# Inner feed-forward groups with the weights stationary and both parts of x moving

## The reference

```python
def rms_norm(x, g):
    y = xf * lax.rsqrt(jnp.mean(xf * xf, axis=-1, keepdims=True) + EPS)
    return (y * g.astype(jnp.float32)).astype(x.dtype)

def swiglu(h, w_gate, w_up, w_down):
    return (jax.nn.silu(h @ w_gate) * (h @ w_up)) @ w_down

    f = swiglu(rms_norm(x, g[0]), w_ffn_gate[layer, 0], ...)
    x = x + 0.5 * rms_norm(f, g[1])
...
    hn = rmsnorm(h, norm2_g[l])
    h = h + jnp.square(jax.nn.relu(hn @ w_ff1[l])) @ w_ff2[l]
```

## Time and profile before

| | before |
|---|---|
| median of 3 runs | 1413.6 us (1412.82 to 1416.67) |
| span of the profiled execution | 1415.0 us (the page gives no other time for it) |
| PE / weight loads busy | 1381.6 / 1130.3 us (98% / 80%) |
| DVE / ACT busy | 808.2 / 682.4 us (57% / 48%) |
| chain that ended last | PE 95%, ACT 3%, DVE 1%, issue 1% |
| DMA | 247.09 MB, 175 GB/s |

### The profile page before, as it was taken

How to read it: one execution, slowest core, us unless ns; L and a number is a source line. 1 busy time by engine, 2 the same in 40 slices (tenths; PEclk the granted TensorE clock), 3 DMA queues, 4 the chain that set the end, 5 groups by cost and what they waited for, 6 DMA issues and landing times.

```text
span 1415.0 us, 17379 instructions
## 1 busy us (share of the span) xinstructions
PE 1381.6 (98%) x6524; PEld 1130.3 (80%) x6524; DVE 808.2 (57%) x886; ACT 682.4 (48%) x873; POOL 36.8 (3%) x100
## 2 busy tenths in 40 slices
PE   6999999999999999999999999999999999999997
PEld 4888888888888888888877788888787678888886
DVE  4444567674455655454568755446676457665543
ACT  5344455454444554433467643445663455553442
POOL 1000000000000000000001100000000000000000
PEclk9999999999999999999999999999999989999999
DMA  7555655546656554565651365555543243565540
GB/s 255 201 184 197 200 190 184 188 144 196 195 179 223 178 185 143 188 197 181 237 184 55 119 199 187 187 199 202 186 177 120 70 171 120 179 222 194 178 163 30
DMA packets 160156, 247.09 MB, mean 175 GB/s; under 512 B 9006, under 2 KB 104424, under 8 KB 160104
## 3 DMA queue, kind: packets, MB, share of 16 engines
q1 hardware_dynamic: 159824, 246.28, 52.3%
q10 hardware_dynamic: 280, 0.10, 0.0%
HBM read 245.30 MB, written 1.05 MB: 174 GB/s over the span
## 4 chain that ended last, share of the span: by engine, by line
PE 95%; ACT 3%; DVE 1%; issue 1%; POOL 0%; DMA 0%; ACTq 0%; POOLq 0%; DVEq 0%
PE GU L527 15%; PE GU L529 15%; PE GU L528 15%; PE DD L527 11%; PE DD L529 11%; PE DD L528 11%; PE GU L592 4%; PE TB L564 3%; PE GU L599 2%; PE TB L720 2%; PE GU L1178 1%; ACT xh L1443 1%; ACT whi L1431 1%; PE DD L1148 0%; DMA sg<-in_hgrn_norm_g 0%
## 5 line engine op out<-in xcount | busy, mean ns | idle before, releaser
L2005 DVE TENSOR_TENSOR wlo<-raw,whi 128x2048 fp32r<-128x2048 f32 (+1 forms) x226 | 513.9, 2282 | 271.3 <-ACT whi L1431 271.2
L1431 ACT ACTIVATE whi<-raw 128x2048 fp32r<-128x2048 f32 (+1 forms) x226 | 429.9, 1909 | 175.8 <-PE DD L529 166.5
L527 PE MATMUL GU<-whi,xh 128*128 128x512 f32 (+1 forms) x944 | 373.0, 395 | 2.9 <-DVE hid L2122 2.9
L529 PE MATMUL GU<-whi,xl 128*128 128x512 f32 (+1 forms) x944 | 367.5, 389 | 0.0
L528 PE MATMUL GU<-wlo,xh 128*128 128x512 f32 (+1 forms) x944 | 366.5, 388 | 0.0
L527 PEld LDWEIGHTS GU<-whi,xh 128*128 128x128 f32 x944 | 177.7, 188 | 39.3 <-issue 4.9
L529 PEld LDWEIGHTS GU<-whi,xl 128*128 128x128 f32 x944 | 177.6, 188 | 37.4
L528 PEld LDWEIGHTS GU<-wlo,xh 128*128 128x128 f32 x944 | 177.8, 188 | 34.6
L527 PE MATMUL DD<-whi,hth 128*128 128x512 f32 x496 | 194.7, 393 | 0.0
L529 PE MATMUL DD<-whi,htl 128*128 128x512 f32 x496 | 193.2, 390 | 0.0
L528 PE MATMUL DD<-wlo,hth 128*128 128x512 f32 x496 | 193.1, 389 | 0.0
(11 more groups left out here) (276 smaller groups left out, 1087.4 us busy)
## 6 DMA issues: line engine op xcount, KB each, us to landing
raw<-in_w_ffn_gate SPq DMA_DIRECT2D x88, 512.0 KB, 4.0
raw<-in_w_ffn_up SPq DMA_DIRECT2D x88, 512.0 KB, 4.9
raw<-in_w_ffn_down SPq DMA_DIRECT2D x88, 512.0 KB, 4.3
raw<-in_w_ff SPq DMA_DIRECT2D x64, 512.0 KB, 4.2
raw<-in_w_in SPq DMA_DIRECT2D x40, 512.0 KB, 4.5
raw<-in_w_conv_in SPq DMA_DIRECT2D x24, 512.0 KB, 4.8
raw<-in_w_kv SPq DMA_DIRECT2D x16, 512.0 KB, 4.7
raw<-in_w_conv_out SPq DMA_DIRECT2D x8, 512.0 KB, 4.8
```

What stands on the lines that cost most here:

```text
L527: pe.matmul(dst, h, w_h, start=start, stop=False)
L529: return pe.matmul(dst, l, w_h, start=False, stop=stop)
L1431: nc.scalar.activation(whi[s][:, 0:size], raw[s][:, 0:size], ACT.Copy).then_inc(hi_done[s], 1)
L2005: nc.vector.tensor_tensor(wlo[s][:, 0:size], raw[s][:, 0:size], whi[s][:, 0:size].bitcast(F32), ALU.subtract).then_inc(lo_done[s], 1)
```

## The change

In groups 1 to 9 of stages 1 to 4 and 1 to 6 of ff the operands change places. A 128x128 piece of the weight tile is stationary, and x moves. `xh` and `xl` now lie side by side in one tensor `xhl`, so that one matmul of 512 columns makes high x high and high x low at once (two sums of 256 columns in one bank), and a second one of 256 columns adds low x high. The hidden channels come out on the partitions, in four quarters of 128 channels: the two banks `GU` (gate) and the two banks `TB` (up). DVE adds each bank's two halves with a reduce over pairs. The hidden values thus are transposed already; `hidden_transposes` remains for group 0 only, and in the last group those of its own values (`tail_transposes`).

The row factor now would be a factor for each column. For the gate it is needed before silu: DVE spreads it (`row_scales`), PE transposes it in step 1 (`row_transposes`), DVE copies it to SBUF (`row_copy`), and `wide_hidden` multiplies with it. For up it is left out, and comes in where DD is read (`rhalf`, the scale of ACT's Square); in ff its square does (`rsq`, relu commutes with it). `hth` is written from `hid` in SBUF when the previous down projection has ended (`wide_hi`, `wide_lo`).

```diff
-        xh = sb("xh", [P, KT, S], F32R)
-        xl = sb("xl", [P, KT, S], F32R)
+        xhl = sb("xhl", [P, KT, 2, S], F32R)
+        xh, xl = xhl[:, :, 0, :], xhl[:, :, 1, :]
...
+                quarter = [GU[:, 0, :], GU[:, 1, :], TB[:, 0, :], TB[:, 1, :]]
...
+                def row_transposes():
+
+                    n.row += 1
+                    pe.wait_ge(spread_ready, n.row)
+                    for t in range(TT):
+                        mm = pe.transpose(DD[:, 0, t * P:(t + 1) * P], spread[:, t, :], ident[:, :])
+                    mm.then_inc(row_ready, 1)
+
+                def wide(f, e, half):
+
+                    wh, wl, cs = view(whi[e.slot], e), view(wlo[e.slot], e), slice(f * P, (f + 1) * P)
+                    for k in range(4):
+                        kk = 4 * half + k
+                        pe.matmul(quarter[f], wh[:, k, cs], xhl[:, kk, :, :].rearrange("p a n -> p (a n)"),
+                                  start=(kk == 0), stop=False)
+                        mm = pe.matmul(quarter[f][:, 0:S], wl[:, k, cs], xh[:, kk, :], start=False, stop=(kk == 7))
+                    return mm
...
                     for b, e in enumerate(es):
-                        pe.wait_ge(t_used[b], d + t0[b] + g + 1)
+                        if g == 0:
+                            pe.wait_ge(t_used[b], t0[b] + 1)
+                        else:
+                            pe.wait_ge(ht_lo[b], d + wide0[b] + g)
...
-                def step(g, at, d=0, static=True):
-
-                    es = ent[at:at + per]
-                    if g == 1:
-                        x_half(gu_banks, es[0], 0, 0, False, read=(gu_used, gu0 + 1), rows=True)
-                    else:
-                        for t in range(TT):
-                            pe.wait_ge(gu_used[t], d + gu0 + g)
-                        x_half(gu_banks, es[0], 0, 0, False, d=d)
-                    hidden_transposes(g - 1, d)
-                    x_half(gu_banks, es[1], 1, 4, True, d=d, done=gu_ready)
-                    down(g - 1, es[2:], d, start=(static and g == 1))
+                def step_1(at):
+
+                    e0, e1, *ds = ent[at:at + per]
+                    pe.wait_ge(gu_used[0], gu0 + 1)
+                    for e in (e0, e1):
+                        pe.wait_ge(lo_done[e.slot], e.raw_before + 1)
+                    wide(0, e0, 0)
+                    wide(0, e1, 1)
+                    hidden_transposes()
+                    if nd == 1:
+                        row_transposes()
+                    pe.wait_ge(gu_used[1], gu0 + 1)
+                    wide(1, e0, 0)
+                    wide(1, e1, 1).then_inc(gu_ready, 1)
+                    for b in range(nd):
+                        pe.wait_ge(t_used[b], t0[b] + 1)
+                    wide(2, e0, 0)
+                    wide(2, e1, 1)
+                    wide(3, e0, 0).then_inc(used[e0.slot], 1)
+                    wide(3, e1, 1).then_inc(used[e1.slot], 1)
+                    if nd == 1:
+                        pe.wait_ge(row_used, n.row)
+                    down(0, ds, 0, start=True)
+
+                def step(g, at, d=0):
+
+                    e0, e1, *ds = ent[at:at + per]
+                    pe.wait_ge(gu_used[0], d + gu0 + g)
+                    pe.wait_ge(lo_done[e0.slot], d + e0.raw_before + 1)
+                    wide(0, e0, 0)
+                    wide(1, e0, 0)
+                    pe.wait_ge(gu_used[1], d + gu0 + g)
+                    wide(2, e0, 0)
+                    wide(3, e0, 0).then_inc(used[e0.slot], 1)
+                    pe.wait_ge(lo_done[e1.slot], d + e1.raw_before + 1)
+                    wide(0, e1, 1)
+                    wide(1, e1, 1).then_inc(gu_ready, 1)
+                    wide(2, e1, 1)
+                    wide(3, e1, 1).then_inc(used[e1.slot], 1)
+                    down(g - 1, ds, d, start=False)
...
-                    hidden_transposes(g - 1, 0)
...
+                step_1(base + 2)
...
+                                     ACT.Square, scale=rcol(FFN_PRE[i], t) if i in FFN_PRE else 1.0,
...
+                def wide_hi(g, ds, d=0):
+
+                    for b, e in enumerate(ds):
+                        act.wait_ge(used[e.slot], d + e.split_before + 1)
+                        act.wait_ge(ht_ready[b], d + wide0[b] + g)
+                        nc.scalar.activation(hth[:, 2 * b:2 * b + 2, :].rearrange("p k n -> p (k n)"), hid[:, b, :],
+                                             ACT.Copy).then_inc(ht_hi[b], 1)
+
+                def wide_gate(g, d):
+
+                    if nd == 1:
+                        act.wait_ge(zg_ready, d + wide0[0] + g)
+                        nc.scalar.activation(sg[:, 0, :], sg[:, 1, :], ACT.Silu).then_inc(silu_done, 1)
...
-                        nc.scalar.activation(sg[:, t, :], GU[:, t, :], ACT.Relu,
-                                             scale=rcol(pre, t)).then_inc(gu_used[t], 1)
...
+                        nc.scalar.activation(sg[:, t, :], GU[:, t, :], ACT.Relu).then_inc(gu_used[t], 1)
...
-                    for q in range(nd):
-                        split(ent[e + q], d)
-                    hidden_hi(g - 1, d)
+                    if g == 1:
+                        for q in range(nd):
+                            split(ent[e + q], d)
+                        hidden_hi()
+                    else:
+                        wide_hi(g - 1, ent[e - per:e - per + nd], d)
+                        for q in range(nd):
+                            split(ent[e + q], d)
                     split(ent[e + nd], d)
-                    gate(g, d)
+                    wide_gate(g, d)
                     split(ent[e + nd + 1], d)
...
-                    ins = nc.vector.scalar_tensor_tensor(out=tmp[:, t, cs], in0=DD[:, 2 * t + nn, :], scalar=HALF[i],
+                    ins = nc.vector.scalar_tensor_tensor(out=tmp[:, t, cs], in0=DD[:, 2 * t + nn, :],
+                                                         scalar=rhalf[:, t:t + 1] if i in FFN_PRE else HALF[i],
                                                          in1=gain[:, i % 2, cs], op0=ALU.mult, op1=ALU.mult)
...
+                def wide_lo(g, d=0):
+
+                    for b in range(nd):
+                        dve.wait_ge(ht_hi[b], d + wide0[b] + g)
+                        nc.vector.tensor_tensor(htl[:, 2 * b:2 * b + 2, :].rearrange("p k n -> p (k n)"), hid[:, b, :],
+                                                hth[:, 2 * b:2 * b + 2, :].rearrange("p k n -> p (k n)").bitcast(F32),
+                                                ALU.subtract).then_inc(ht_lo[b], 1)
+
+                def wide_sum(dst, banks, done):
+
+                    return nc.vector.tensor_reduce(dst.rearrange("p (f n) -> p f n", f=2),
+                                                   banks[:, :, :].rearrange("p f (a n) -> p f n a", a=2), AX.X, ALU.add)\
+                        .then_inc(done, 1)
+
+                def wide_hidden(g, d):
+
+                    dve.wait_ge(gu_ready, d + gu0 + g + 1)
                     if nd == 1:
-                        dve.wait_ge(sg_done[t], d + sg0 + g + 1)
-                        nc.vector.scalar_tensor_tensor(out=hid[:, t, 0:FG], in0=GU[:, t, FG:512], scalar=rcol(pre, t),
-                                                       in1=sg[:, t, 0:FG], op0=ALU.mult, op1=ALU.mult)\
+                        wide_sum(sg[:, 1, :], GU, gu_used[0])
+                        dve.wait_ge(gu_used[0], d + gu0 + g + 1)
+                        z = sg[:, 1, :].rearrange("p (f n) -> p f n", f=2)
+                        nc.vector.tensor_tensor(z, z, rrow.unsqueeze(1).broadcast_to([P, 2, S]), ALU.mult).then_inc(zg_ready, 1)
+                        dve.wait_ge(used[later1.slot], d + later1.split_before + g)
+                        wide_sum(hid[:, 0, :], TB, gu_used[1])
+                        dve.wait_ge(gu_used[1], d + gu0 + g + 1)
+                        dve.wait_ge(silu_done, d + wide0[0] + g)
+                        nc.vector.tensor_tensor(hid[:, 0, :], hid[:, 0, :], sg[:, 0, :], ALU.mult).then_inc(ht_ready[0], 1)
+                    else:
+                        for b, banks in ((0, GU), (1, TB)):
+                            if b:
...
+                            nc.vector.scalar_tensor_tensor(out=hid[:, b, :], in0=sg[:, b, :], scalar=0.0, in1=sg[:, b, :],
+                                                           op0=ALU.max, op1=ALU.mult).then_inc(ht_ready[b], 1)
...
+                def row_scales():
+
+                    c = ncol[pre]
+                    if nd == 1:
+                        nc.vector.tensor_copy(spread, rs[:, c:c + 2].unsqueeze(2).broadcast_to([P, TT, P])).then_inc(spread_ready, 1)
+                        chain(nc.vector.tensor_scalar(rhalf, rs[:, c:c + 2], HALF[i], None, ALU.mult))
+                    else:
+                        chain(nc.vector.tensor_tensor(rsq, rs[:, c:c + 2], rs[:, c:c + 2], ALU.mult))
+
+                def row_copy():
+
+                    if nd == 1:
```

(60 more changed lines are left out.)

107 lines of the change are left out of this document (59 added, 48 removed).

## The result

The changed kernel takes **1423.1 us** (median of 4 runs, 1421.71 to 1427.15) against 1413.6 (1412.82 to 1416.67): a ratio of 1.006, interval 1.0042 to 1.0078. It is slower by 0.6%, outside the range given (1401 to 1420), and 13.6 us above the forecast of 1409.5. The profiled execution took 1421.7 us, with a span of 1419.8; before, that span was 1415.0.

A forecast was written before the change was run, and what follows sets the result against it. PE was taken to bound the kernel, through matmul spacing and its pauses. Inner groups -15.6, stage starts +10.2 and clock +1.3 summed to -4.1 us; off the 1413.6 us median, 1409.5 us, range 1401 to 1420.

The forecast's parts named there:

- Part 1: Inner groups on PE: extra matmul time +6.1 us, removed transposes -22.6, new row-factor transposes +0.9; -15.6 us in all.
- Rival 1: Inner groups on PE: the short 256-column matmul costs more, up to 0.1281 us, giving 1423 us; chance 0.13.
- rival 3: Inner groups on PE: additional weight loads are not overlapped, 74 us more, 1483 us; chance 0.02.
- Part 2: Hidden values between groups: DVE's sums and the row-factor product hide behind PE with at least 5 us slack; nothing.
- Part 3: Start of each stage: PE's group 1 waits for both gate tiles' low parts, behind row_scales on DVE; +10.2 us.
- Part 4: Granted clock around PE's lengthened stage-start pauses: time lost at half clock, +1.3 us in all.

The follow-up runs named there:

- x5_padded: Changed kernel with the 256-column matmuls of the inner groups widened to 512 columns, as many matmuls and weight loads; 1561.7 us (one run).
- x4_before_wait: Kernel before plus only PE's wait for the second tile's low part ahead of group 1 and DVE's two row_scales operations; 1430.2 us, ratio 1.0111.
- x7_early: Changed kernel with group 1 doing all four quarters of its first half after waiting for the first gate tile alone; 1414.0 us, 0.9986 of before.
- x1_runs4: Changed kernel with four 512-column matmuls, then four 256-column ones, in place of turns; 1425.3 us, 1.0055 of before.
- x2_runs16: Changed kernel with sixteen long, then sixteen short matmuls in each half from group 2 on, runs of four in group 1; 1420.8 us, 1.0035 of before.
- x3_long_only: Changed kernel without the inner groups' 256-column matmuls (weights' low part times x's high part left out); 1264.7 us (one run).
- x8_early_runs32: x7_early with 16 long, 32 short, 16 long matmuls in each group; 1405.7 us, 0.9924 of the kernel before.

## Why the prediction was wrong

**Part 1 failed, and in one term.** The step reads "32 x (0.2267 + 0.1179) = 11.03 us". It priced the short matmul with care, and took 0.2267 for the long one from a stretch in which every matmul has the same length. In turn with short ones it costs 0.354 - 0.118 = 0.236. The first part is 11.29 us and not 11.03, and the down projection behind it 16.793 - 11.29 = 5.50 and not 5.44, since its first matmuls follow a short one. Together that is 0.323 us a group, 37 x 0.323 = 12.0 us in the looped groups. Group 1 and the last group of each stage add some 0.7, so that Part 1 came to -2.9 us and not -15.6: **12.7 us** dearer. The transposes did go, with the 0.474 us put down to them; the alternation took nearly all of it back.

With the other parts as measured below the sum is -2.9 + 9.9 + 0.9 = +7.9 us. The profiled executions, with the 4.5 us of before's own slow stretch taken off, differ by 1419.8 - 1410.5 = 9.3. The remaining 1.4 us lie in small pieces outside of these groups, where the prediction put nothing; no run looks into them.

**Rival 1 had the size and the sign, and the wrong place.** It said that alternation might be dear, "which the trace shows nowhere", at up to 1423 us, but put the price on the short matmul, which came out at 0.1175. That its 10 ns for each short one come so near to the 10 ns that each long one had is luck. It got 0.13, since the argument against it was about 256 columns and about loads, and said nothing on a change of length. The trace of before did hold a hint: there too, from the second 512-column matmul behind the transposes on (in stage 2 at 319.13 us), nine follow each other at 0.224 to 0.236 us, before they settle at 0.2267. I had averaged over the 72 and put the rest down to the transposes.

**Loads in the open (rival 3) are excluded.** 88 matmuls of 512 columns, each with a load of its own, take 0.2267 us each (x5_padded); the 16 additional loads cost nothing. The rule of the Trainium skill ("TensorE: Matmul & The Clock Gate", Part 3, What overlaps and what doesn't), that a load overlaps only where the row group differs, would have added the 74 us of rival 3; no run here agrees with it.

**Part 2 was right**: PE has no idle time in any inner group, and the reduces took 1.22 us as taken. The order on DVE wasn't the one laid out, though nothing hung on it.

**Part 3 was right.** Group 1 of stage 1 starts 33.46 - 30.72 = 2.74 us later than before. In stage 2 it is 318.78 - 313.02 = 5.76, of which 3.93 was there already at the stage's first matmuls (311.41 against 307.48): 1.83. In the same way the others give 0.78, 2.54 and 1.99: 9.9 where the sum said 10.2. row_scales costs 0.39 us (30.63 to 31.02), taken as 0.45. x4_before_wait shows the same price put on alone (10 us in its quickest execution), and x7_early its removal. The idle times are shorter than these shifts, since idle time is counted from the end of the last record, which lies behind the time at which the next could have started.

**Part 4** said +1.3, and the profile after shows 0.9. It was no constant: behind the same pauses of stage 4 and ff the clock fell twice more in the profiles of x1_runs4, x2_runs16 and x3_long_only, once more in that of x5_padded, and not at all in those of x4_before_wait and after. So in these profiles the term lay between 0.9 and some 4.3 us (0.9 + 3.4), by the mean clocks it was larger in x4_before_wait's slowest executions, and the runs do not settle its mean.

What remains open is why a change of length is dear, and why it takes nine matmuls to settle behind strict alternation or the transposes, and five behind a run of short ones. Shown is that it is so, for how many matmuls, and that it needs neither these operands, nor the number of loads, nor the kernel's form.

## What to carry to other kernels

A matmul's price read from a stretch of equal ones holds for such a stretch. Before a change mixes lengths, look in the trace for a place where lengths change already, and read the distances one by one behind it. Where lengths must be mixed, do all of one length first: here that turned a change worth next to nothing in the inner groups into 0.24 us for each. And a wait moved to the head of a block on the bounding engine cost its full length here, so put there only the tile that the first matmuls read.

## What was not expected of the hardware

Equal matmuls, each with its weight load, follow each other at 0.2267 us (512 columns, in the down projection and throughout the inner groups of x3_long_only and x5_padded) and 0.120 us (256, from the third of a row of 16 or 32 on). Where long ones follow a row of short ones, the first five have 0.228 to 0.236 us (x2_runs16 and x8_early_runs32), and in strict alternation they never settle (0.232 to 0.241 from one to the next, mean 0.236). In these groups it is the long one that pays: the short one had 0.115 to 0.118 in the mean beside long ones, a little less than in a row of its own.
